# A two-layer decoder step on one core: the first weights asked for before the prompt's first rows, and seven small reorders

## What is computed

```
h = rmsnorm(x, norm_pre[l]);  z = h @ w_in[l]        # 1024 x 4040: q k v qi ki wi ga xb gb u vc gc
score = sum_h relu(qi_h . ki) * wi_h                 # indexer; causal; the best 128 (prompt) or 256 (sample) keys
ya = softmax(q . k over the chosen keys) @ v         # sample: 2048 past positions in 16 pages of K and V per sequence
yb = (trailing means of xb - xb) @ pool_w * scale    # windows 2, 4, 8, 16
yc = u * (tril(sgu_w) @ layernorm(vc) + sgu_b)
x  = x + rmsnorm([ya*silu(ga), yb*silu(gb), yc*silu(gc)] @ w_out[l], norm_post[l])
```

## Time and profile before

| | |
|---|---|
| median of three runs | 947.67 us |
| profiled execution | 947.23 us |
| its span | 945.5 us |
| PE busy | 923.1 us, 98% |
| DVE busy | 534.5 us, 57% |
| ACT busy | 309.9 us, 33% |
| mean traffic | 217 GB/s |

### The profile page before, as it was taken

One profiled execution on the slowest core, in us unless ns is written; L12 is line 12 of the kernel. 1 busy time (PEld: TensorE's weight loads), 2 busy tenths in 40 slices (PEclk: granted clock), 3 DMA queues, 4 the chain that ended last, 5 costly groups with the idle time before them and its releaser, 6 DMA issues.

```text
span 945.5 us, 20317 instructions
## 1 busy us (share of the span) xinstructions
PE 923.1 (98%) x7052; PEld 477.4 (50%) x7052; DVE 534.5 (57%) x1624; ACT 309.9 (33%) x670; POOL 270.0 (29%) x481
## 2 busy tenths in 40 slices
PE   6999999999999999999999999999999999999996
PEld 4534444444455556654564444544445555565543
DVE  6349999579952224324353699967898313242332
ACT  3121232331242446433232212333222424563312
POOL 5831223223222222312932022323232222221130
PEclk9999999999999999999999999999999999999999
DMA  9862777677857665755884157767677667566561
GB/s 322 153 218 97 252 252 259 212 266 245 290 197 247 215 223 180 263 205 192 228 232 149 64 199 252 258 234 259 226 260 250 223 227 246 196 220 244 180 191 56
DMA packets 93665, 205.21 MB, mean 217 GB/s; under 512 B 16055, under 2 KB 28566, under 8 KB 93570
## 3 DMA queue, kind: packets, MB, share of 16 engines
q0 software_dynamic: 38576, 122.63, 38.3%
q1 hardware_dynamic: 49218, 76.87, 24.7%
q10 hardware_dynamic: 5776, 4.46, 1.8%
HBM read 193.88 MB, written 10.14 MB: 216 GB/s over the span
## 4 chain that ended last, share of the span: by engine, by line
PE 90%; DMA 3%; ACT 2%; ACTq 1%; issue 1%; DVE 1%; SPq 0%; POOLq 0%; POOL 0%; DVEq 0%
PE bank L1583 42%; PE bank L1959 11%; PE bank L1566 6%; PE bank L1637 6%; PE bank L1600 6%; PE bank L1868 2%; PE bank L1831 2%; PE bank L1749 2%; PE bank L1660 2%; PE bank L1691 2%; DMA pg<-in_cache_k_dram 2%; PE bank L1784 1%; ACTq L657 1%; PE bank L1877 1%; DMA pg<-in_cache_v_dram 1%
## 5 line engine op out<-in xcount | busy, mean ns | idle before, releaser
L1583 PE MATMUL bank<-wr,ht 128*128 128x512 f32 (+1 forms) x1024 | 434.6, 578 | 0.1
L1583 PEld LDWEIGHTS bank<-wr,ht 128*128 128x128 f32 x1024 | 189.7, 190 | 213.1 <-issue 200.7
L739 POOL DMA_DIRECT2D wr<-in_w_in_dram x47 | 34.7, 737 | 278.4 <-PE bank L1583 215.7
L756 POOL DMA_DIRECT2D pg<-in_cache_v_dram x128 | 69.2, 540 | 147.4 <-PE bank L1637 121.8
L756 POOL DMA_DIRECT2D pg<-in_cache_k_dram x128 | 69.5, 543 | 74.2 <-PE bank L1600 53.5
L1180 DVE TENSOR_SCALAR_CACHE_REDUCE r<-r,sel_i 128x1088 bf16<-128x1088 f32 x62 | 83.3, 1344 | 1.7
L1566 PE MATMUL bank<-wr,ht 128*32 128x256 f32 (+1 forms) x1152 | 65.3, 379 | 0.2 <-issue 0.2
L1600 PE MATMUL bank<-pg,qbx 128*32 128x256 f32 x1024 | 62.9, 382 | 1.5 <-DMA pg<-in_cache_k_dram 0.6
L1637 PE MATMUL bank<-pg,rs 128*32 128x256 f32 x1024 | 62.1, 382 | 1.0 <-DMA pg<-in_cache_v_dram 0.9
L1959 PE MATMUL bank<-wr,qt 128*128 128x512 f32 x128 | 58.4, 599 | 0.0
L1959 PE MATMUL bank<-wr,ht 128*128 128x512 f32 x128 | 57.5, 592 | 0.0
(11 more groups left out here) (272 smaller groups left out, 1102.4 us busy)
## 6 DMA issues: line engine op xcount, KB each, us to landing
pg<-in_cache_k_dram SPq DMA_DIRECT2D x128, 256.0 KB, 5.3
pg<-in_cache_k_dram POOLq DMA_DIRECT2D x128, 256.0 KB, 5.9
pg<-in_cache_v_dram SPq DMA_DIRECT2D x128, 256.0 KB, 5.3
pg<-in_cache_v_dram POOLq DMA_DIRECT2D x128, 256.0 KB, 5.9
wr<-in_w_in_dram POOLq DMA_DIRECT2D x40, 512.0 KB, 4.2
wr<-in_w_in_dram POOLq DMA_DIRECT2D x3, 2048.0 KB, 10.7
wr<-in_w_out_dram POOLq DMA_DIRECT2D x8, 512.0 KB, 4.1
wr<-in_w_out_dram POOLq DMA_DIRECT2D x2, 2048.0 KB, 8.9
```

What stands on the lines that cost most here:

```text
L739: pool.dma_start(W[n % 2][:, k, d0:d0 + w], src[k.start * P:k.stop * P, c0:c0 + w].rearrange("(k p) n -> p k n", p=P))\
L756: pool.dma_start(PG[2 * gi + e], cache[l, bass.ds(nos[2 * gi + e], 1), :, :].rearrange("o p n -> p (o n)"))\
L1583: mm = pe.matmul(b[0:m, 0:w], HT[:, k, rt * P:rt * P + m], W[n % 2][:, k, 0:w], start=(k == 0), stop=(k == KC - 1))
```

## The change

The list of steps is put in another order at these places, and three waits are changed.

- SP asks for the first weights in front of the prompt's tile 0. The list begins with the norms of the sample and of tile 0, the sample's transposes, the norm of tile 1, and then the sample's projection; the transposes of tiles 0 and 1 and the norms of tiles 2 and 3 stand behind it; the transposes of tile 3 one tile later.
- The first page steps K of pair 0 stand behind tiles 9, 10, 11, 12 instead of 10, 11, 12, 13; the transposes of qi and of the indexer keys ("kip") come with them; the transposes of k one tile later.
- The logits of heads (1, 3) stand in front of page step (K, 3, 0).
- Mask piece (3, 2) stands a tile earlier.
- The sample's gating stands behind tile 41 instead of 38. ACT's first output copy waits for the prompt's gating alone, no more for the sample's and for its store.
- The second layer's norm of tile 2 stands in front of output tile (3, 0) instead of behind it.
- SP waits for the last page group's use before it stores the first rows of y.

```
-LOGITS_FIRST = (25, 26, 27, 28, 32, 34, 35, 36, 39)
+LOGITS_FIRST = (25, 26, 27, 28, 32, 33, 34, 35, 36, 39)
...
-            (3, (36, 0), 2, (37, 0), (38, 3)))
+            (2, ((29, 4, 3), (30, 0, 2)), (30, 3)), (3, ((36, 0, 2), (36, 4, 1), (37, 0, 2)), (38, 3)))
...
-PLACES = [10, 11, 12, 13, 14, 16, 17, 18, 20, ...
+PLACES = [9, 10, 11, 12, 14, 16, 17, 18, 20, ...
...
-        pre = [("norm", 0, ST), ("norm", 0, 0), ("xT", 0, ST), ("xT", 0, 0), ("norm", 0, 1), ("norm", 0, 2)]
-        put(0, FRONT, ("xT", 1), ("norm", 3))
+        pre = [("norm", 0, ST), ("norm", 0, 0), ("xT", 0, ST), ("norm", 0, 1)]
+        put(0, FRONT, ("xT", 0), ("norm", 2), ("xT", 1), ("norm", 3))
         put(1, FRONT, ("xT", 2))
-        put(2, FRONT, ("xT", 3))
+        put(3, FRONT, ("xT", 3))
...
+    put(9, FRONT, ("T", "q", ST), ("kip",), ("T", "qi", 0))
+    put(11, FRONT, ("sgus",))
+    for rt in range(1, PT_TILES):
+        put(9 + rt, FRONT, ("T", "qi", rt))
...
+        put(at["q", rt] + 2, FRONT, ("T", "q", rt))
+        put(at["k", rt] + 3, FRONT, ("T", "k", rt))
...
-    put(38, COLS, ("sg", ST))
+    put(41, COLS, ("sg", ST))
...
-            put(last[rt] + 1, BACK, ("norm", rt), layer=l + 1)
+            put(last[rt] + (rt != 2), BACK, ("norm", rt), layer=l + 1)
...
             load_rows(ST)
-            load_rows(0)
             d0 = 0
             for c0, w in CHUNKS[0][1]:
                 sp.dma_start(W[0][:, :, d0:d0 + w], ...).then_inc(w_first_in, 16)
                 d0 += w
+            load_rows(0)
...
+            sp.wait_ge(group_used, page_used(*PAGES[-1]))
             for rt in RES[-1]:
...
-                    act.wait_ge(y_ready, 3 * (l + 1))
-                    act.wait_ge(st_cv, 16 * (l + 1))
+                    act.wait_ge(y_ready, done("sg", l, 1))
```

More of the change, by code:

```diff
@@ L162 @@
             (40, 4, 3, (0,)), (41, 4, 3, (1,)), (42, 4, 3, (2,)), (43, 4, 3, (4, 3)))
-MASKS_AT = ((0, (18, 0), 3, (18, 4), (18, 4)), (1, (20, 0), 3, (20, 4), (21, 3)), (2, (29, 4), 3, (30, 0), (30, 3)),
-            (3, (36, 0), 2, (37, 0), (38, 3)))
-PLACES = [10, 11, 12, 13, 14, 16, 17, 18, 20, 21, 22, 23, 24, 25, 26, 27, 28, 30, 31, 32] + list(range(33, 45))
+MASKS_AT = ((0, ((18, 0, 3), (18, 4, 2)), (18, 4)), (1, ((20, 0, 3), (20, 4, 2)), (21, 3)),
+            (2, ((29, 4, 3), (30, 0, 2)), (30, 3)), (3, ((36, 0, 2), (36, 4, 1), (37, 0, 2)), (38, 3)))
+PLACES = [9, 10, 11, 12, 14, 16, 17, 18, 20, 21, 22, 23, 24, 25, 26, 27, 28, 30, 31, 32] + list(range(33, 45))
 PI_PLACES = [(18, 1), (18, 3), (19, 1)] + [(n, part) for n in (20, 21, 22, 23) for part in (1, 3)] + [(24, 3)]
@@ L212, in _layer @@
     put(at["kg", ST], FRONT, ("wexp",))
-    put(12, FRONT, ("sgus",))
-    for rt in range(PT_TILES):
-        put(10 + rt, FRONT, ("T", "qi", rt))
+    put(9, FRONT, ("T", "q", ST), ("kip",), ("T", "qi", 0))
+    put(11, FRONT, ("sgus",))
+    for rt in range(1, PT_TILES):
+        put(9 + rt, FRONT, ("T", "qi", rt))
     put(s0, BACK, *[("S", 0, p) for p in range(PAIRS)], ("S", 2, 0), ("H", 0), ("H", 2), *[("S", 1, p) for p in range(PAIRS)])
     put(s0, BACK, ("rope",) + tiles[s0][2:])
-    put(11, FRONT, ("kip",))
     put(s0 + 1, FRONT, ("wt",))
     put(s0 + 1, COLS, ("H", 1))
-    put(at["q", ST] + 1, FRONT, ("T", "q", ST))
     put(at["k", ST] + 2, ROWS_A, ("T", "k", ST))
-    for name in ("q", "k"):
-        for rt in range(PT_TILES):
-            put(at[name, rt] + 2, FRONT, ("T", name, rt))
+    for rt in range(PT_TILES):
+        put(at["q", rt] + 2, FRONT, ("T", "q", rt))
+        put(at["k", rt] + 3, FRONT, ("T", "k", rt))
     put(14, BACK, ("silu", "ys"))
@@ L260, in _layer @@
             put(n, part, *[("turn", p, j) for j in js])
[L261 to L264, removed]
+    for p, pieces, (n_exp, part_exp) in MASKS_AT:
+        j = 0
+        for n, part, k in pieces:
+            put(n, part, *[("mk", p, i) for i in range(j, j + k)])
+            j += k
+        put(n, part, ("mx", p))
+        put(n_exp, part_exp, ("exp", p))
     pairs = [(i, c) for i in range(1, PT_TILES) for c in range(NC4)]
```

## The result

The changed kernel takes 948.87 us (median of 22 runs, 947.25 to 951.15), the kernel before, run beside it on the same chip, 947.18 us (22 runs, 945.53 to 949.01). The ratio is 1.0019, 95% interval 1.0011 to 1.0026: slower by about 1.8 us. The interval does not hold 1, but the difference is no larger than the 1.9 us that the prediction counted as no change. The profiled execution has a span of 947.1 us, against 945.5 before.

The account below looks back on a forecast made before the run. PE, busy 98% of the span, was taken as the bound, so start delays count in full. Start +4.3, reorders -0.5, -1.3, -0.6 and -0.9 sum to +1.0 us on the 947.67 median: 948.7, range 945.2 to 951.2.

Parts of the forecast that it names:

- Steps 1 to 5: Start: prompt tile 0 lands 4.1 us late, delaying the sample's projection and first prompt projection; tile "kg 3" +4.0 us.
- Step 3: Start: the sample's projection, with matmuls at the slow pace, was to last 4.25 us.
- Step 6: Start: ACT's key loads run late, so its copy of "kg 2" holds PE; price 0.4 us, bounds 0 and 1.5.
- Earlier pages and transposes at the mask rows: Scoring to first mask matmuls: DVE sets the tempo, so moving them gains 0 in both layers, bounds -0.6 and +0.3.
- Heads' logits: In front of page step (K, 3, 0): two logits matmuls fill PE's wait on ACT's copy of gr, -0.5 us.
- Mask piece: Piece (3, 2) one tile earlier removes PE's wait for a DVE bank: -1.3 us in two layers, bounds 0 and -1.3.
- Norm of tile 2: Between the layers: the norm in front of "out 3 0" removes PE's 0.59 us wait for it, -0.6 us.
- Wait in front of the stores: At the end: with SP's stores held back, the last page group lands in time for PE, -0.9 us.
- Rival C: Start as forecast, but new mask bank, gating bank or page waits keep away half of 3.3 us: 950.3; chance 0.12.
- A: Start: prompt rows hardly late, tile 0 landing near 7.0 as engines serve both requests side by side: 944.7; chance 0.12.
- D: Start costs only 2.5 us or less, as PE reaches full pace sooner and copies overlap: 946.9; chance 0.10.
- B: Start: ACT becomes the bound, PE waits for its copies, scoring starts 6 to 7 us late: 950.9; chance 0.16.

Follow-up runs that it names:

- experiment 1: Kernel before with only the changed start (weights asked for ahead of prompt tile 0, new list): 951.6 us against 947.3, ratio 1.0045.
- experiment 3: Changed kernel with the norm of prompt tile 0 put behind the sample's transposes: 943.98 us against 947.3 for the kernel before, ratio 0.9967.
- experiment 4: Kernel before with only the load of prompt tile 0 moved behind the weights, one profiled execution: scoring at 52.49, +3.94 us.
- experiment 7: Changed kernel with the logits of heads (1, 3) put back behind page step (K, 3, 0), one execution: first-layer stretch 32.36 us against 31.93.
- experiment 10: Changed kernel without SP's wait before the final stores, one execution: 39.2 us from the last value page step to the end instead of 38.5.
- experiment 6: Changed kernel with the second layer's norm of tile 2 put back, one execution: second scoring at 514.38, 0.33 us earlier.
- experiment 8: Changed kernel, tile 0's norm behind the sample's transposes, POOL's key loads one tile later, second-layer logits put back: 943.87 us against 946.57, ratio 0.9967.
- experiment 5: Kernel before with only the start's new list, loads as before, one profiled execution: scoring at 50.26, +1.71 us.
- experiment 9: Kernel before with only the changed start, tile 0's norm behind the sample's transposes: 947.07 us against 947.2, ratio 1.0001.

## Why the prediction was right

**Its time and sign of no change.** 948.7 was forecast and 948.87 measured, on the slow edge of "no difference". Part of that closeness is luck: the sum said +1.0 and was set on the 947.67 of three runs; the kernel before is at 947.18 over 22, and the difference measured side by side is 1.8. The sum is also the balance of misses: the mask pieces and the logits brought 0.8 more than forecast, the norm 0.3 less, and a page took 0.8 that it does not have. The terms:

- *Steps 1 to 5, the start, +4.3:* right, step by step. Tile 0 landed at 10.67 (10.5 said), the sample's projection began at 14.07 (13.8) and lasted 4.60 (4.25), the first prompt projection came at 21.20 (21.1), tile "kg 3" at 41.2 (41.1), the scoring 4.14 us late. Experiments 1, 3 and 4 show that DVE's place at the norm, as the text had it, is the cause. Step 3 was sized too small: all 64 matmuls at the slow pace, 480 ns each, make 4.60 us; the transposes behind it took 2.5 us instead of 3.0 and made up for it. That all 64 were slow is a matter of the execution: behind the same wait the projection took 4.34 us in experiment 1 and 4.05 in experiment 7, with means of 462 and 436 ns. Two slips of the working do not change its outcome: the old starts are 11.35 and 16.27 in the earlier trace rows, not 11.42 and 16.43, and 4.0 and 0.4 make 4.4, not 4.3.
- *Step 6, ACT +0.4:* 0.1 to 0.3. ACT got its first keys at 23.91 as said (23.9), but its second eight requests took 5.61 us and not 6.80, so the copy of "kg 2" began at 43.97. In experiment 10 they took 7.12 us and PE waited 0.28: the mechanism is there, and its size is chance.
- *Earlier pages and transposes at the mask rows, 0:* right, as far as traces can tell. The waits moved to L1852, 0.8 and 0.6 us, and what stands behind did not come sooner; it came 0.3 us later in the first layer and 0.05 in the second, within the scatter of that stretch.
- *Heads' logits −0.5:* 0.46 and 0.45 in the changed kernel's table, in two layers; the term took 0.5 for both together, so it was half of what there is. *Mask piece −1.3:* 0.84 a layer, 1.7, over the bound of 1.3. No run has this edit alone, but from the last key page step to behind the mask pieces pass 12.77 us in both layers of all five kernels with the old order and 11.93 in those of all seven with the new one.
- *Sample gating 0:* +0.1 a layer, at the upper bound given.
- *Norm of tile 2 −0.6:* this step failed. The wait went, as said, in every trace with the norm moved, and it is worth 0.6 us where nothing follows; but the next thing that is late, the first weights of the second layer, was not named. The change lets POOL ask no earlier for them, so PE comes for them 9.0 us after the request instead of 9.5 (experiment 6), and in this execution 0.3 is left of the 0.6 at the second scoring.
- *Wait in front of the stores −0.9:* 1.1 (experiment 10: 0.7 in a direct comparison; 0.5 to 1.5 over the six traces without the wait).
- *Not in the sum:* the page wait of 0.9 us at (K, 3, 1) of the second layer. It is there in some traces and not in others (0.47 in experiment 7, 0.19 in experiment 3, none in experiments 6 and 8). Rival C had the kind right, with a page on its list and weights not, but half was too much: the reorders brought 2.6 in this trace, and 1.1 more without the 0.3 lost at the weights and the 0.8 at the page. That the two waits belong to the new start is not shown; they come and go between executions.

**The rivals.** A is out: tile 0 landed at 10.67, behind the weights and not beside them. D is out by 4.14 against 2.5. B is out at this place, as the copy of "kg 2" never held PE by more than 0.3 us, but its kind of price is real: in experiments 5 and 9 ACT's requests cost 1.2 us.

The Trainium skill, TensorE: Matmul & The Clock Gate, Part 1, has it that the array is slow until it has been busy and that the number of slow matmuls differs from run to run. By the first, the matmuls of step 3 should be slow after 5.4 us of idleness, as they were (480 ns against 304). The second agrees too: with the same 64 matmuls after 0.6 to 0.7 us of idleness, experiment 3 has 481 ns and experiment 9 has 421, the granted clock shown as 1.00, the 2.4 GHz level, in both.

## What to carry to other kernels

A load that is put later need not cost anything by itself: look at which engine reads it first, and what stands behind that instruction in its list. Here one norm in front of a copy turned a useful order of loads into 4 us, and putting it one place further removed the whole loss (ratio 0.9967 instead of 1.0019) without touching a load. And when a change has two halves of opposite sign, time each alone before judging the whole: these reorders were 3.4 us faster, hidden under a start that was 4.3 us slower. Where an edge is met by half a microsecond, as with the weights between the layers, a gain just in front of it is not yet a gain.

## What the runs showed of the hardware

- *Requests cost the engine that issues them a time that varies.* The same eight key loads on ACT took from 5.61 to 7.25 us in the traces, at places 26 to 38 us into the kernel, and in the two traces where the first of these groups took over 7.1 us (experiments 5 and 9) PE waited 1.2 us for the copy behind it.
- *Landing varies as much.* The same 1,024 KB of weights, asked for at the same place, landed after 7.7 to 10.0 us in eleven traces; 256 KB pages made PE wait 0.2 to 1.25 us at steps that other executions of nearly the same kernel passed without a wait.
- *Single executions scatter by more than a reorder is worth.* The kernel before took 945.53 to 949.01 us in 22 runs, where the first three lay within 0.6 us. What the trace shows of the start (4 us) stood above this; pieces of 0.5 us were read only where several traces agreed.
